# Five rotations by transfer and 512-column up projections in a two-block transformer kernel

## The reference

```python
def squared_relu_mlp(h, w1, w2):
    return jnp.square(jax.nn.relu(h @ w1)) @ w2
```

```python
def apply_rope(t, cos, sin):
    t1, t2 = jnp.split(t, 2, axis=-1)
    rot = jnp.concatenate([-t2, t1], axis=-1)
    return (t * cos + rot * sin).astype(t.dtype)

def mixer_c(h, cos, sin, w_in, w_out):
    q, k, v = jnp.split(h @ w_in, 3, axis=-1)
    q = apply_rope(q.reshape(Bn, S, C_HEADS, HEAD_DIM), cos, sin)
    k = apply_rope(k.reshape(Bn, S, C_HEADS, HEAD_DIM), cos, sin)
    ...
    return moba_attention(q, k, v) @ w_out
```

## Time and profile before

| | us |
|---|---|
| median of 3 runs | 1499.44 |
| lowest, highest | 1496.66, 1501.49 |
| profiled execution, its own time | 1497.52 |
| its span, first to last instruction | 1495.7 |
| TensorE busy in it | 1368.4 (91%) |
| VectorE busy | 969.2 (65%) |
| ScalarE busy | 599.2 (40%) |
| mean granted clock of TensorE | 0.955 |

### The profile page before, as it was taken

The page is one execution under the profiler, slowest core; times in us unless marked ns, Lnnn a source line. Parts: engine busy times, 40 slices in busy tenths (PEclk is TensorE's granted clock), DMA queues, the critical chain, the costliest instruction groups (busy, mean ns, idle before and its releaser), DMA issues.

```text
span 1495.7 us, 22547 instructions
## 1 busy us (share of the span) xinstructions
PE 1368.4 (91%) x8866; PEld 1191.7 (80%) x8866; DVE 969.2 (65%) x1289; ACT 599.2 (40%) x803; POOL 13.3 (1%) x24
## 2 busy tenths in 40 slices
PE   5986979999899789999979987999997999999997
PEld 1763679998788578999879986999987777899996
DVE  2767579777887568666676874755567545575554
ACT  2434344334344433433354322543346453443332
POOL 0000000000000000000000000000000000000000
PEclk7998989999999789999989998999999999999999
DMA  9744439787294235656535321455543420455540
GB/s 385 273 171 138 173 109 350 285 308 268 73 335 149 92 113 213 233 202 215 177 131 184 132 85 57 172 194 181 186 167 113 141 72 14 170 211 194 181 158 28
DMA packets 44688, 262.90 MB, mean 176 GB/s; under 512 B 5063, under 2 KB 6727, under 8 KB 18890
## 3 DMA queue, kind: packets, MB, share of 16 engines
q1 hardware_dynamic: 31520, 216.88, 40.1%
q10 hardware_dynamic: 13102, 45.09, 8.4%
HBM read 260.89 MB, written 1.05 MB: 175 GB/s over the span
## 4 chain that ended last, share of the span: by engine, by line
PE 78%; DVE 12%; ACT 5%; issue 3%; DMA 2%; SPq 0%; POOL 0%; DVEq 0%; ACTq 0%; POOLq 0%
PE banks L512 22%; PE banks L513 22%; PE banks L514 22%; DMA A<-ada_w 2%; DVE w_lo L1570 2%; PE banks L719 2%; PE banks L1036 2%; PE banks L676 1%; ACT w_hi L1075 1%; ACT A L1091 1%; PE banks L622 1%; PE banks L658 1%; DVE mx L1666 1%; PE banks L904 1%; PE banks L689 1%
## 5 line engine op out<-in xcount | busy, mean ns | idle before, releaser
L1570 DVE TENSOR_TENSOR w_lo<-raw,w_hi 128x2048 fp32r<-128x2048 f32 x193 | 439.8, 2287 | 187.6 <-ACT w_hi L1075 184.4
L1075 ACT ACTIVATE w_hi<-raw 128x2048 fp32r<-128x2048 f32 x193 | 368.7, 1913 | 242.8 <-PE banks L514 217.6
L512 PE MATMUL banks<-hT_hi,w_hi 128*128 128x256 f32 x1432 | 413.6, 289 | 6.0 <-DVE hT_lo L1559 3.9
L513 PE MATMUL banks<-hT_lo,w_hi 128*128 128x256 f32 x1432 | 410.0, 286 | 0.0
L514 PE MATMUL banks<-hT_hi,w_lo 128*128 128x256 f32 x1432 | 409.8, 286 | 0.0
L512 PEld LDWEIGHTS banks<-hT_hi,w_hi 128*128 128x128 f32 x1432 | 279.5, 195 | 12.4 <-issue 7.3
L513 PEld LDWEIGHTS banks<-hT_lo,w_hi 128*128 128x128 f32 x1432 | 279.7, 195 | 3.1 <-issue 0.7
L514 PEld LDWEIGHTS banks<-hT_hi,w_lo 128*128 128x128 f32 x1432 | 279.5, 195 | 0.0
L512 PE MATMUL banks<-w_hi,R 128*128 128x512 f32 (+1 forms) x592 | 232.2, 392 | 4.2 <-DVE R L1559 2.1
L513 PE MATMUL banks<-w_lo,R 128*128 128x512 f32 (+1 forms) x592 | 230.3, 389 | 0.0
L514 PE MATMUL banks<-w_hi,R 128*128 128x512 f32 (+1 forms) x592 | 229.6, 388 | 0.0
(11 more groups left out here) (227 smaller groups left out, 1260.0 us busy)
## 6 DMA issues: line engine op xcount, KB each, us to landing
raw<-stream SPq DMA_DIRECT2D x193, 1024.0 KB, 4.9
A<-ada_w ACTq DMA_DIRECT2D x73, 512.0 KB, 5.5
A<-ada_w SPq DMA_DIRECT2D x6, 1024.0 KB, 16.5
raw<-ada_w SPq DMA_DIRECT2D x3, 1024.0 KB, 7.4
A<-ln_g ACTq DMA_DIRECT2D x4, 512.0 KB, 3.6
A<-ln_b ACTq DMA_DIRECT2D x4, 512.0 KB, 5.4
A<-ada_w SPq DMA_DIRECT2D x1, 1536.0 KB
A<-x_t SPq DMA_DIRECT2D x2, 512.0 KB, 21.9
```

The lines of the kernel that those rows point to most:

```text
L512: pe.matmul(o, lh, rh, start=start, stop=False, skip_group_check=True)
L513: pe.matmul(o, lh, rl, start=False, stop=False, skip_group_check=True)
L1075: act.activation(w_hi[:, s, :], raw[:, s, :], ACT.Copy).then_inc(hi_done, 1)
L1570: v.tensor_tensor(w_lo[:, s, :], raw[:, s, :], w_hi[:, s, :], ALU.subtract).then_inc(lo_done, 1)
```

## The change

`hT_hi` and `hT_lo` become two halves of one tensor `hT`. In pairs 2 to 15 of every MLP, the two products with `w_hi` become one with 512 columns, hT_hi and hT_lo side by side; the product of `w_lo` with `hT_hi` stays and is added to the first 256 columns. Each half a has a bank of its own now (banks 0 and 1 for even pairs, 2 and 3 for odd ones), so ScalarE copies the second halves of two banks to SBUF, VectorE adds the first halves (semaphore `u_sum`), and then does max with 0 and multiplication in one instruction. The products for the gate go to banks 0 and 1.

In the second attention, rotations 10 to 14 (`SWAPPED`) have no permutation product. The sync queue moves the four blocks of 32 partitions crosswise from the copied fill to the place of the result; VectorE multiplies the copy by cos, waits for the transfers, multiplies what they brought by sin and adds. The transfers stand in the sync queue ahead of the loads of units CU+14 to CU+18, whose loop is cut open for that. The steps get another order: `collect` of a head pair follows the next score, `rope` stands ahead of the ada multiply-add, and iteration 1 has none of these, so that one more is done at the end.

```diff
--- before.py
+++ after.py
@@ -95,8 +95,8 @@
         w_hi = sb("w_hi", [P, SLOTS, UNIT], f32r)
         w_lo = sb("w_lo", [P, SLOTS, UNIT], f32r)
         X = sb("X", [P, TT, D])
-        hT_hi = sb("hT_hi", [P, KT, SEQ], f32r)
-        hT_lo = sb("hT_lo", [P, KT, SEQ], f32r)
+        hT = sb("hT", [P, 2, KT, SEQ], f32r)
+        hT_hi, hT_lo = hT[:, 0], hT[:, 1]
...
@@ -351,12 +353,14 @@
                                             for kind in ("score", "exps", "spread", "collect"))
             for j in range(8):
                 u, c = CU + 4 + j, j - 3
-                s += (score(c) + exps(c) if c >= 0 else []) + fills(u, "T", "h", "rope", [C_TMP]) + rest(u - 1 + SLOTS)
-                s += (spread(c) if c >= 0 else []) + [("ahead", u)] + some(1)
+                s += score(c) if c >= 0 else []
+                s += collect(c - 1) if c >= 1 else []
+                s += (exps(c) if c >= 0 else []) + fills(u, "T", "h", "rope", [C_TMP]) + rest(u - 1 + SLOTS)
+                s += (spread(c) if c >= 0 else []) + [("ahead", u)]
                 if j:
                     s += rope(j - 1)
-                s += collect(c) if c >= 0 else []
-            s += score(5) + exps(5) + rope(7) + rest(CU + 15) + score(6) + exps(6) + spread(5) + score(7) + spread(6) + exps(7)
+                s += some(j != 1)
+            s += score(5) + collect(4) + exps(5) + rope(7) + rest(CU + 15) + score(6) + exps(6) + spread(5) + score(7) + spread(6) + exps(7)
             s += collect(5) + spread(7) + some(1) + collect(6) + some(1) + collect(7) + [("rows", 1, 0)]
             return s + downs(CU + 12, [0, 1, 2, 3], {0: some(1), 1: some(len(parts))})
 
@@ -437,6 +441,13 @@
         STEPS += bound(5, "rms", M2 + 31, own("kv_in"), own("mla"), lead=(ML,)) + mla_steps()
         STEPS += bound(6, "rms", ML + 17, own("mlp", 8)) + [("final_row",), ("mlp", 3, M3, None, None)]
         STEPS += bound(7, "final", M3 + 31, None)
+
+        rope_to = [step[1:] for step in STEPS if step[0] == "rope"]
+        SWAPPED = range(10, 15)
+
+        def halves_of(r):
+
+            return halves_in[r % 2], 64 * (1 + sum(q % 2 == r % 2 and q < r for q in SWAPPED))
 
         def T_unit(u0, k):
 
@@ -478,10 +489,29 @@
             for u in (6, 7):
                 sp.wait_ge(lo_done, u + 1 - SLOTS)
                 load(u, u - SLOTS)
-            with sp.Fori(2, UNITS // SLOTS) as i:
-                for s in range(SLOTS):
-                    sp.wait_ge(lo_done, SLOTS * i + (s + 1 - SLOTS))
-                    load(SLOTS * i + s, s)
+            def loads(first, last):
+
+                with sp.Fori(first, last) as i:
+                    for s in range(SLOTS):
+                        sp.wait_ge(lo_done, SLOTS * i + (s + 1 - SLOTS))
+                        load(SLOTS * i + s, s)
+
+            def swap(r):
+
+                tmp, _, to, w = rope_to[r]
+                sp.wait_ge(turn_f, r + 1)
+                for at in range(0, P, 32):
+                    sp.dma_start(A[at:at + 32, to:to + w], A[at ^ 32:(at ^ 32) + 32, tmp + 512 * (r % 2):][:, 0:w]).then_inc(
+                        halves_of(r)[0], 16)
+
+            first, last = (CU + 12) // SLOTS, (CU + 18) // SLOTS + 1
+            loads(2, first)
+            for u in range(SLOTS * first, SLOTS * last):
+                if 8 + u - (CU + 12) in SWAPPED:
+                    swap(8 + u - (CU + 12))
+                sp.wait_ge(lo_done, u + 1 - SLOTS)
+                load(u, u % SLOTS)
+            loads(last, UNITS // SLOTS)
             for u in range(UNITS // SLOTS * SLOTS, UNITS):
                 sp.wait_ge(lo_done, u + 1 - SLOTS)
                 load(u, u % SLOTS)
@@ -745,10 +775,11 @@
                 f0, p0 = n["fill"], n["plain"]
 
                 def up(k, kp, u, s):
-                    if isinstance(k, int) and k < 2:
+                    first = isinstance(k, int) and k < 2
+                    if first:
                         claim((f0 + kp) % 2)
                     else:
-                        pe.wait_ge(fill_read, k + (p0 - 1))
+                        pe.wait_ge(u_sum, k + (PAIRS * m - 1))
                     pe.wait_ge(lo_done, u + 1)
                     wh = w_hi[:, s, :].rearrange("p (k n) -> p k n", k=KT)
                     wl = w_lo[:, s, :].rearrange("p (k n) -> p k n", k=KT)
@@ -762,9 +793,16 @@
                         if late and (a, kt) == (1, 0):
                             group_x(2, 1, 1, True)
                             n["y"] += 2 * TT
-                        last = mm3(B[(f0 + kp) % 2][:, 256 * a:256 * a + 256],
-                                   wh[:, kt, P * a:P * a + P], wl[:, kt, P * a:P * a + P],
-                                   hT_hi[:, kt, :], hT_lo[:, kt, :], kt == 0 and not (late and a), kt == KT - 1)
+                        if first:
+                            last = mm3(B[(f0 + kp) % 2][:, 256 * a:256 * a + 256],
+                                       wh[:, kt, P * a:P * a + P], wl[:, kt, P * a:P * a + P],
+                                       hT_hi[:, kt, :], hT_lo[:, kt, :], kt == 0 and not (late and a), kt == KT - 1)
+                            continue
+                        bank = B[2 * kp + a]
+                        pe.matmul(two(bank), wh[:, kt, P * a:P * a + P], hT[:, :, kt, :], start=kt == 0, stop=False,
+                                  skip_group_check=True)
+                        last = pe.matmul(bank[:, 0:256], wl[:, kt, P * a:P * a + P], hT_hi[:, kt, :], start=False,
+                                         stop=kt == KT - 1, skip_group_check=True)
                     last.then_inc(unit_done, 1)
 
                 def dn(k, kp, u, s, first=False):
...
@@ -777,6 +815,9 @@
                 pe.wait_ge(y_read, n["y"])
                 pe.wait_ge(gate_read, n["gates"])
                 dn(0, 0, D_unit(u0, 0), D_unit(u0, 0) % SLOTS, first=True)
+                pe.wait_ge(fill_read, p0 + 2)
+                for b in (2, 3):
+                    claim(b)
                 with pe.Fori(0, LOOPS) as i:
                     for j in range(2):
...
-                        mm = pe.matmul(B[2 + h][:, :], ones[:, :], gate_r[:, 512 * h:512 * h + 512], start=True, stop=True)
+                        mm = pe.matmul(B[h][:, :], ones[:, :], gate_r[:, 512 * h:512 * h + 512], start=True, stop=True)
                     mm.then_inc(gate_ps, 1)
                     n["gates"] += 1
-                    held[3] = (gate_read, n["gates"])
                 weights(D_unit(u0, k))
                 pe.wait_ge(u_ready, PAIRS * m + k)
                 down_last(D_unit(u0, k - 1), [(u_hi[j], u_lo[j]) for j in ((k - 1) % 2, k % 2)],
                           lambda: pe.wait_ge(u_ready, PAIRS * m + k + 1))
                 n["fill"] += PAIRS
                 n["plain"] += PAIRS
-                for j in range(2):
-                    held[(f0 + j) % 2] = (fill_read, n["plain"] - 1 + j)
+                for b in range(4):
+                    held[b] = (gate_read, n["gates"]) if s_gate and b < 2 else (u_sum, PAIRS * (m + 1) - 1 + b // 2)
 
             def bias_rows(b, row, n_):
 
@@ -898,6 +939,9 @@
                 elif kind == "fill":
                     fill(*a[0:6])
                 elif kind == "rope":
+                    if n["turn"] in SWAPPED:
+                        n["turn"] += 1
+                        continue
                     pe.wait_ge(turn_f, n["turn"] + 1)
                     claim(2)
                     buf, w = a[0] + 512 * (n["turn"] % 2), a[3]
...
@@ -1160,7 +1204,10 @@
                     act.wait_ge(unit_done, u + 1)
                     if not (isinstance(k, int) and PAIRS * m + k < 2):
                         act.wait_ge(u_ready, k + (PAIRS * m - 1))
-                    act.activation(u_f[:, kp, :], B[(f0 + kp) % 2][:, :], ACT.Relu).then_inc(fill_read, 1)
+                    if isinstance(k, int) and k < 2:
+                        act.activation(u_f[:, kp, :], B[(f0 + kp) % 2][:, :], ACT.Relu).then_inc(fill_read, 1)
+                        return
+                    act.activation(two(u_f[:, kp, :]), banks[:, 2 * kp:2 * kp + 2, 256:512], ACT.Copy).then_inc(fill_read, 1)
 
                 relu(0, 0, T_unit(u0, 0))
                 ahead(T_unit(u0, 0))
...
@@ -1595,8 +1642,17 @@
 
                 def square(k, kp, step, u_free):
                     v.wait_ge(fill_read, k + (p0 + 1))
-                    v.tensor_tensor(u_f[:, kp, :], u_f[:, kp, :], u_f[:, kp, :], ALU.mult).then_inc(v_step, 1)
-                    v.wait_ge(v_step, step + 1)
+                    if isinstance(k, int) and k < 2:
+                        v.tensor_tensor(u_f[:, kp, :], u_f[:, kp, :], u_f[:, kp, :], ALU.mult).then_inc(u_sum, 1)
+                        v.wait_ge(u_sum, k + (PAIRS * m + 1))
+                        step -= 1
+                    else:
+                        v.tensor_tensor(two(u_f[:, kp, :]), banks[:, 2 * kp:2 * kp + 2, 0:256], two(u_f[:, kp, :]),
```

(15 more changed lines are left out.)

8 lines of the change are left out of this document (6 added, 2 removed).

## The result

The changed kernel took 1486.5 us (median of 4 runs, 1484.6 to 1488.7) against 1500.5 (4 runs) of the kernel before on the same chip: a ratio of 0.990, with a 95% interval of 0.989 to 0.992, or 14 us less. The forecast was 1477, 20.7 less, with a range of 1472 to 1487. So the direction was right and two thirds of the gain came. The time lies at the upper edge of the range, beside the 1486.5 of rival A. Of the 9.7 us over the sum's 1476.8, 3 are the base (the forecast started from one execution of 1497.5, and the median is 1500.5) and 6.7 are gain that did not come. The profiled execution took 1484.6 us with a span of 1482.8.

What follows compares the result with a forecast made beforehand. TensorE's products were taken to bound the MLPs, and its waits for rotations to add time in the second attention. Terms -10.5, +1.4, -4.75, -1.8, -2.0, -2.7, -0.3 sum to -20.7 us, from 1497.5 to 1476.8, said as 1477; range 1472 to 1487.

Steps and rivals of the forecast that it cites:

- rival A: MLPs: the fixed part does not go with the number of products, only 0 to 2 us gained; about 1486.5 us, chance 0.15.
- Up projections: Pairs 2 to 15 of each MLP: a group takes 0.3477 us instead of 0.3594, over 896 groups -10.5 us.
- The ends of the MLPs: Last down projection of the third and fourth MLP: one more VectorE operation, not hidden, 0.73 us each, +1.4 us.
- -4.75: Second attention: five permutation products, rotations 10 to 14, leave TensorE at 0.95 us each, -4.75 us.
- -1.8: Second attention: rotations 11 and 13 no longer end behind the next score, so the two smaller waits go, -1.8 us.
- -0.3: Second attention: moved collect gives 0.80 us once, but rotation 15 comes some 0.5 us later; net -0.3 us.
- First score and slow clock: Second attention: new order brings the first score 2.0 us earlier; the slow-clock stretch behind it goes, -2.7 us.
- rival B: Second attention gives less: clock falls anyway, VectorE sets the pace, or swaps land late; about 1481 us, chance 0.16.
- three signs: Prediction wrong if VectorE waits for a transfer, clock is 0.50 behind the first score, or MLP loops stay as long.
- Transfers: Second attention: a swap takes between 2 and 10 us, 6 assumed, hidden with 2 us to spare.
- C: Up projections: the 512-column product streams more slowly on two strips than on one; 1505.5 us at 0.26 us each, chance 0.03.
- D: Second attention: swaps land too late and stop VectorE mid-rotation; 1507 us with all late, about 1489 with two, chance 0.04.

Runs made afterwards that it cites:

- the kernel with one strip: The changed kernel with hT laid out so that hT_hi and hT_lo of one slice lie side by side; 1484.5 us, ratio 0.988.
- the order alone: Only the new order of the second attention's steps against the kernel before, permutation products and MLPs as before; 1499.4 us, ratio 1.000.
- the second trace of the changed kernel: The changed kernel measured once more, nothing changed, against the kernel before on the same chip; 1483.2 us, ratio 0.989.

## Why the prediction was partly right, step by step

**Up projections: the step that was too large.** Forecast -10.5 us, measured -6.2. The count (896 groups) and the place were right. What failed was taking the 512-column distance from a row of products that all have 512 columns, and the 256-column one likewise, for a sequence in which they take turns: a group costs 0.3525 us and not 0.3477. The two bounds that I had set out, strips and a cost that is not one of each product, were the wrong ones to look at; the nearest was in rival A, which tied the fixed part to "the switch of strip or bank", but strip and bank are excluded by their runs, and it is the width. Rival A had 1486.5 us and, as its sign, a 512-column distance of 0.24, and both are there, yet not for its reason: the 256-column distance is 0.12 and the group is shorter by 0.0069, and A took the whole 9.5 us from the MLPs, where 4.3 were missing. The rest is the attention's, the base of the forecast and the spread of measurements. That the time met A's is chance. The Trainium skill, "TensorE: Matmul & The Clock Gate", section "Back-to-back issue gap", has a formula for isolated products (columns / 2.4 plus 2.5 ns). An estimate from it for a group is 325 ns; the traces do not agree, in turn (352.5) or in rows (347.5).

**The ends of the MLPs.** Forecast +1.4 us with a gap of 0.73, measured two of 0.58: the mechanism, and nearly the size.

**Five products less and two waits less: -4.75, -1.8 and -0.3.** The terms have to be laid on the stretches in which they stand. Four of the five products and both waits lie between the second score and the sixth: forecast 3.8 + 1.8 = 5.6 us, and the traces have 41.7 (456.83 to 498.53) and 37.1 (455.07 to 492.16), 4.6 less. The missing 1.0 is four iterations at 9.27 and not 9.0, because score, mask and collect in a row take 1.98 us (464.34 to 466.32) where the forecast summed 1.81, and the spread ahead of a score takes 1.44 and not 1.34. The durations were read in places where other products follow. The -0.3 was 0.80 less and 0.5 more. The 0.80 comes between the first score and the second, where no collect stands any more; the 0.5 between the sixth and the seventh, 5.31 us (492.16 to 497.47) for 4.81 (498.53 to 503.34), as forecast. VectorE was not the pace, as forecast. What the prediction did not see is that the two parts of the edit need each other: in the old order the product covered the collect's wait for ScalarE's copy, and with the product kept the collect gave the rotation time ahead of the score. The sum came out all the same because both parts were in.

**First score and slow clock: -2.0 and -2.7. The terms that were too large in the attention.** In the changed kernel's trace the first score comes 4.06 us after the last product with the permutation matrix, and before it was 4.68, so 0.6 and not 2.0 came. Behind the wait of 3.04 us the clock was at 0.50, and the stretch to the second score is 3.05 us shorter. Forecast for it were 0.95 for the product, 0.80 for the collect and 2.7 for the clock. Product and collect came; the products behind the score take 6.34 us (447.30 to 453.64) for 7.73, so the clock gave 1.4 of its 2.7. The trace of the kernel with grouped products shows the step as it was forecast:

```profile
436.74 1.02 PE L959 MATMUL banks<-A,perm 128*128 128x512 f32 x2
...
439.47 0.93 PE L688 MATMUL banks<-A 64*128 64x128 f32 x8 [1.71 <-DVE A L1892]
```
```profile
438.00:440.00 2.00, 0.53 (x7) 1.00 0.94 283
440.00:442.00 2.00, 2.00 (x19) 1.00 0.88 315
```

There the wait is 1.71 us, as forecast, the score comes after 2.73 us, and the clock stays. That the modulation's weights come in time is what the forecast took for granted, and of the seven traces with both parts of the new attention only this one bears it out: in the other six the first score waits 2.17 to 3.04 us and the clock falls behind it, also in the kernel with one strip:

```profile
444.53 0.94 PE L688 MATMUL banks<-A 64*128 64x128 f32 x8 [2.20 <-DVE A L1881]
```

The forecast leaned on one place where the clock stayed at 1.00 behind 2.50 us. The length of a wait doesn't decide it alone: 1.71 us were followed by 1.00 and by 0.50 within one trace (the order alone, above). This was rival B, at 1481, and it happened in part. Two of the three signs by which the prediction said it would be wrong are there with it: the clock at 0.50 behind the first score, and VectorE's wait for a transfer. What is left of the attention is its end, for which the sum had no term: from the seventh score to the last collect are 21.1 us (497.47 to 518.55) for 22.5, 1.4 less. The last three collects ran at the full clock, 0.87, 0.90 and 0.87 us for 1.55 each. That is luck: in the second trace of the changed kernel all three take 1.55 us, and the stretch 23.7 (495.33 to 519.05).

**Transfers.** Median 3.9 us to landing for an assumed 6 of a whole swap; but the first swap took 11.3 us and not 2 to 10, and VectorE waited 0.56 us for it. By the prediction's own sign (VectorE never waits there) this is a miss, though a cheap one: no score of the changed kernel waited for it. Where the first score came early, in the grouped kernel, VectorE waited 1.77 us for the same swap and a later score 0.29. The other four swaps never made VectorE wait. Rivals C and D, with their prices, did not happen.

By the terms, then: -6.2 + 1.2 - 9.9 = -14.9 us, and -14.4 and -16.2 were measured. Grouping the products by width gives a kernel of 1479.9 us, the lowest median of all here, 19.5 us under that of the kernel before and 17.7 by the ratio.

## What to carry to other kernels

Take the distance of two products from a row where they stand in that order, not from two rows of one kind each; and where widths must be mixed, try them in groups: 0.08 us came back in 11.1 by order alone. Before removing an instruction from a chain that is read in order, ask which wait it covered, on its own engine: the five products gave 2 us alone and, with the collect moved, 9.9. Where the DMA engines are full, look at several traces of both kernels before an idle time is put down to an edit, or to chance: here three of seven had it on one side and none of four on the other. And a clock that stayed up behind one wait is no price for the next one.

## What the runs showed of the hardware

A 512-column product followed by a 256-column one and so on costs 0.3525 us for the two, grouped 0.3475, with the same weights, operands and banks; an operand in one strip or two made no difference, nor did a change of bank from group to group. Single transfers of 64 KB between partitions took 3.9 us in the median beside weight loads with 4.9, and a swap of four in a row 11.3 from the copy of its source. Waits of 2.17 to 3.04 us ahead of the first score were followed by a granted clock of 0.50 in six traces; a wait of 1.71 us was followed by 1.00 in two places and by 0.50 in a third, so its length alone does not tell.
